# Splitting two row tiles of x first, residual copies on ScalarE, ten convolution taps moved

## The chip, the core and the metric

The kernel runs on one core of one Trainium2 chip. The metric is the device time of one execution in microseconds, median of the runs shown. TensorE, VectorE, ScalarE, GpSimd and SyncE run their own instruction streams and meet at semaphores; a transfer is issued on the queue of SyncE (SP) or ScalarE.

## What is computed

Two blocks follow each other on x of 256 tokens by 2048 channels, all in float32. The first block has two layers, and only it is touched by the change:

```python
hn = _rmsnorm(h, norm_g[i])
u = hn @ w_in[i]
a_val, a_glu, a_z, q, k, v, b_z = jnp.split(u, offs, axis=-1)
ya = _conformer_conv(a_val, a_glu, conv_w[i], ...)   # GLU, depthwise conv of width 31, LayerNorm, swish
ya = ya * silu(a_z)
yb = _window_attention(q, k, v, bias_band, sink[i]) * silu(b_z)
h = h + concatenate([ya, yb]) @ w_out[i]
e = _rmsnorm(p[i] @ w_pe[i], pe_g[i])
h = h + e * sigmoid(h @ w_pg[i])
```

The second block is one layer of forgetting attention and one of windowed attention, each with an input and an output projection.

## The kernel before

The activations lie channel-major: 16 row tiles of 128 channels by 256 tokens. Every product of float32 matrices is made of three reduced ones: x is split into a high and a low half (`a_hi`, `a_lo`; the next operand is `b_hi`, `b_lo`), and so is every weight (`w_hi`, `w_lo`). A weight is streamed in pieces of 256 rows by 512 columns through a ring of four slots (`RING`). For each piece, in this order: SP loads it into `stage` once the split of four pieces earlier is done (`load`, L286); ScalarE rounds it to `w_hi` (`rounded`, L1522); VectorE subtracts to get `w_lo` (`split`, L893); TensorE runs 24 matmuls over it (`gemm_piece`, L495, or L506 for the transposed kind). Eight pieces make a chunk of 512 output columns. The first block takes 156 pieces a layer: 11 input chunks (four of value and GLU columns, keys and values, two of q, two of gates, two of `z`), 4 pieces for `w_pe`, 8 x 4 for `w_out`, 4 x 8 for `w_pg`. All products take 577 pieces.

Each engine's program is a list written by hand: `chunk(hooks)` runs eight pieces and puts other work ("hooks") after piece i. VectorE's and ScalarE's chunk calls run three pieces behind the start of TensorE's chunks, since three splits come before the first call: VectorE's first call covers pieces 3 to 10, the next 11 to 18, and so on.

Start: ScalarE fetches `ident` and the norm gains, SP fetches x in four parts (`x_part`, L303) between the first weight loads, then 14 small constant arrays (`consts`, L308), then goes on loading weights. TensorE transposes x, four tiles to a part (`turn_x`, L665), parts 0 and 1 ahead of the first matmul, parts 2 and 3 inside the first chunk. ScalarE scales and rounds a tile from PSUM (`x_high`, L1531), VectorE makes the low half (`x_low`, L1073) and copies the part to the residual `h` (`x_new`, L1041 and L1045). TensorE waits for `operand_ready` ahead of every second piece. The sums of squares of h go ScalarE, VectorE (L948 to L955), TensorE (`stats`, L560), VectorE (`var`, L933), GpSimd (`inverse_root`, L1855 and L1857: a power, then a diagonal), TensorE (`spread_rs`, L572), VectorE (`take_rs`).

The depthwise convolution is VectorE's: 31 taps for 8 channel tiles are 248 steps of 128 x 256 (`taps`, L1139; the first tap of a tile is L1135), strewn between the splits. `conv_chunk(hooks, counts)` puts `counts[i]` taps after the split of its i-th piece and never more than are left (`spent`); after each pair of tiles `ln_add` (L1123) adds them to the mean. The last one releases TensorE's `ln_sum` (L719) in the second quarter of the attention half of `w_out`. The calls' counts stand in the diff. `evac` is the hook that takes a finished chunk out of PSUM, `gated` and `low_att` finish one half of the attention.

## Time and profile before

| | |
|---|---|
| median of 3 runs | 1775.8 us (1775.53 to 1776.24) |
| profiled execution, its own time | 1774.86 us |
| its span | 1773.1 us |
| TensorE busy | 1753.8 us (99%), 14349 matmuls |
| VectorE busy | 1309.7 us (74%) |
| ScalarE busy | 900.5 us (51%) |
| GpSimd busy | 38.1 us (2%) |
| from HBM | 320.4 MB, 182 GB/s over the span |

All times are from one profiled execution. A line of the timeline says when the first instruction of a group began, how long the group took, engine, line, operation, output and inputs, how many, and in brackets the idle time of the engine before it with what ended that. "L893" is line 893 of the kernel. Matmuls overlap, and their ends are modelled, so TensorE's busy share is high even where it runs below its peak; the starts of matmuls are the safer measure.

### The profile page before, as it was taken

The numbers are of one execution on the slowest core, as the hardware profiler recorded it, in microseconds if no ns is written. First come the engines' busy times: TensorE is split into PE (matmuls) and PEld (weight loads), VectorE is DVE, ScalarE is ACT, GpSimd is POOL, SyncE is SP. The second block draws the span as 40 slices with busy tenths as digits, with TensorE's granted clock in tenths as the row PEclk, the third lists the DMA queues.
The fourth block names the chain that finished last, engine by engine and source line by source line (L and its number), as shares of the span: only waits on it lengthen the run. The fifth ranks groups of instructions, "written<-read, shape, count | busy, mean of one in ns | idle before, by whom it ended". The sixth has DMA issues, their size and how long they took to land.

```text
span 1773.1 us, 35684 instructions
## 1 busy us (share of the span) xinstructions
PE 1753.8 (99%) x14349; PEld 1685.0 (95%) x14349; DVE 1309.7 (74%) x2087; ACT 900.5 (51%) x1326; POOL 38.1 (2%) x48
## 2 busy tenths in 40 slices
PE   8999999999999999999999999999999999999997
PEld 7999999999999999999999899999989999999886
DVE  7899899977679987998777765556565556666754
ACT  5433665545533465456565463545455443665553
POOL 0000000000000000000000110100100000000000
PEclk9999999999999999999999999999999999999999
DMA  7666655555666664556566666665655556555553
GB/s 233 188 206 195 191 145 177 195 186 194 196 188 204 195 201 145 157 194 197 180 200 184 206 200 181 192 187 181 193 159 167 191 179 192 156 158 172 168 193 131
DMA packets 200082, 326.07 MB, mean 184 GB/s; under 512 B 14911, under 2 KB 66319, under 8 KB 199821
## 3 DMA queue, kind: packets, MB, share of 16 engines
q1 hardware_dynamic: 197085, 320.85, 58.2%
q10 hardware_dynamic: 2864, 3.36, 0.6%
q8 instruction: 94, 1.54, 0.4%
q14 instruction: 39, 0.32, 0.1%
HBM read 320.42 MB, written 2.69 MB: 182 GB/s over the span
## 4 chain that ended last, share of the span: by engine, by line
PE 94%; DVE 4%; SPq 1%; ACT 0%; DMA 0%; issue 0%; DVEq 0%; ACTq 0%
PE g L495 75%; PE g L506 11%; PE att L596 2%; PE att L640 2%; PE att L620 2%; DVE w_lo L893 1%; DVE cacc L1139 1%; SPq L308 0%; PE att L495 0%; DMA stage<-in_w_in_dram 0%; PE att L784 0%; SPq L286 0%; ACT w_hi L1522 0%; PE att L572 0%; PE att L853 0%
## 5 line engine op out<-in xcount | busy, mean ns | idle before, releaser
L893 DVE TENSOR_TENSOR w_lo<-stage,w_hi 128x1024 fp32r<-128x1024 f32 x577 | 704.5, 1229 | 380.0 <-ACT w_hi L1522 379.1
L1522 ACT CAST w_hi<-stage 128x1024 fp32r<-128x1024 f32 x577 | 599.5, 1050 | 618.1 <-PE g L495 410.1
L495 PE MATMUL g<-a_hi,w_hi 128*128 128x256 f32 x2496 | 705.2, 283 | 3.0 <-DVE w_lo L893 2.0
L495 PE MATMUL g<-a_lo,w_hi 128*128 128x256 f32 x2496 | 695.9, 279 | 0.0
L495 PE MATMUL g<-a_hi,w_lo 128*128 128x256 f32 x2496 | 695.8, 279 | 0.0
L495 PEld LDWEIGHTS g<-a_hi,w_hi 128*128 128x128 f32 x2496 | 469.5, 188 | 13.0 <-issue 8.6
L495 PEld LDWEIGHTS g<-a_lo,w_hi 128*128 128x128 f32 x2496 | 472.7, 189 | 0.0
L495 PEld LDWEIGHTS g<-a_hi,w_lo 128*128 128x128 f32 x2496 | 469.2, 188 | 0.5 <-issue 0.2
L495 PE MATMUL g<-b_hi,w_hi 128*128 128x256 f32 x1440 | 404.4, 281 | 0.1
L495 PE MATMUL g<-b_lo,w_hi 128*128 128x256 f32 x1440 | 401.2, 279 | 0.0
L495 PE MATMUL g<-b_hi,w_lo 128*128 128x256 f32 x1440 | 401.2, 279 | 0.0
L495 PEld LDWEIGHTS g<-b_hi,w_hi 128*128 128x128 f32 x1440 | 270.6, 188 | 3.9 <-issue 2.9
L495 PEld LDWEIGHTS g<-b_lo,w_hi 128*128 128x128 f32 x1440 | 271.9, 189 | 0.0
L495 PEld LDWEIGHTS g<-b_hi,w_lo 128*128 128x128 f32 x1440 | 271.5, 189 | 0.1
L1139 DVE SCALAR_TENSOR_TENSOR cacc<-glu,cw,cacc 128x256 f32<-128x256 f32 x480 | 201.8, 478 | 0.2
L1531 ACT ACTIVATE u<-u,nbias 128x128 f32<-128x128 f32 (+1 forms) x192 | 88.1, 460 | 5.8 <-DVE nbias L1372 5.8
L1587 ACT COPY u<-att 128x384 f32<-128x384 f32 (+1 forms) x96 | 44.6, 516 | 53.4 <-PE att L620 53.4
L506 PE MATMUL g<-w_hi,a_hi 128*128 128x512 f32 (+1 forms) x192 | 68.9, 359 | 0.0
L506 PE MATMUL g<-w_lo,a_hi 128*128 128x512 f32 (+1 forms) x192 | 68.1, 355 | 0.0
L506 PE MATMUL g<-w_hi,a_lo 128*128 128x512 f32 (+1 forms) x192 | 67.8, 353 | 0.0
L506 PE MATMUL g<-w_hi,b_hi 128*128 128x512 f32 (+1 forms) x156 | 58.2, 373 | 0.0
L506 PE MATMUL g<-w_hi,b_lo 128*128 128x512 f32 (+1 forms) x156 | 57.5, 368 | 0.0
(230 smaller groups left out, 1359.9 us busy)
## 6 DMA issues: line engine op xcount, KB each, us to landing
stage<-in_fox_w_in_dram SPq DMA_DIRECT2D x128, 512.0 KB, 3.7
stage<-in_w_in_dram SPq DMA_DIRECT2D x112, 512.0 KB, 3.8
stage<-in_swa_w_in_dram SPq DMA_DIRECT2D x72, 512.0 KB, 3.8
stage<-in_w_in_dram SPq DMA_DIRECT2D x128, 256.0 KB, 3.1
stage<-in_w_out_dram SPq DMA_DIRECT2D x64, 512.0 KB, 4.3
stage<-in_w_pg_dram SPq DMA_DIRECT2D x64, 512.0 KB, 4.0
stage<-in_fox_w_out_dram SPq DMA_DIRECT2D x32, 512.0 KB, 4.3
stage<-in_swa_w_out_dram SPq DMA_DIRECT2D x32, 512.0 KB, 4.7
```

Of the source, the lines that this page charges most:

```text
L495: mm = pe.matmul(acc[:, j * S:(j + 1) * S], w[:, slot, c0 + j * P:c0 + (j + 1) * P], xx[:, k, :], start=st and m == 0 and j % 2 == 0, stop ...
L506: mm = pe.matmul(acc[:, at:at + width], xx[:, k, b * P:(b + 1) * P], w[:, slot, col:col + width], start=st and m == 0 and (kind == "N" or ...
L596: mm = pe.matmul(score_bank(j, len(pairs))[:, c:c + n], q_of(j, b), keys(j)[:, 0:n], start=b == 0, stop=True, skip_group_check=True)
L620: mm = pe.transpose((TB, SB)[j % 2][:, n * P:(n + 1) * P], uw[:, j, c + kb * P:c + (kb + 1) * P], ident[:, :])
L640: mm = pe.matmul(dst[half(j):half(j) + HD, at + first * P:at + S], values(j, kb), uw[:, j, n * P:(n + NB - first) * P], start=i % 2 == 0 a ...
L893: dve.tensor_tensor(w_lo[:, slot, :], stage[:, slot, :], w_hi[:, slot, :].bitcast(F32), ALU.subtract).then_inc(*t.inc("w_split"))
L1139: dve.scalar_tensor_tensor(out=cacc[:, c, :], in0=src, scalar=cw[:, c, l, k:k + 1], in1=cacc[:, c, :], op0=ALU.mult, op1=ALU.add).then_inc ...
L1522: act.copy(w_hi[:, slot, :], stage[:, slot, :]).then_inc(*t.inc("w_rounded"))
L1531: return act.activation(out, in_, func, **kw).then_inc(*t.inc(name))
L1587: act.copy(uw[:, j, 0:n], (TB, SB)[j % 2][:, 0:n]).then_inc(*t.inc("t_free"))
```

## The change

It has five parts.

1. x. Part 0 is fetched in two halves of two row tiles (`x_in0`, `x_in0b`). They are transposed, rounded and split separately, VectorE signals `operand_ready` after every two tiles, and TensorE waits for it ahead of every piece of the first chunk ("each"). TensorE runs nine matmuls on `ones` while nothing has arrived yet. The gains are fetched ahead of the identity.
2. The order on VectorE and ScalarE. The second weight piece is rounded and split between parts 0 and 1 of x.
3. Residual. Parts 0 and 1 of x, eight tiles, are copied to `h` by ScalarE, four copies of 128 x 512 (`x_keep`), behind the third rounded piece and ahead of the fetch of `p_in`. TensorE's `turn_x(2)` and `turn_x(3)` wait for them.
4. Taps, early. The third, fourth and fifth calls of `conv_chunk` lose 3, 5 and 3 taps.
5. Taps, late. The two calls with `normed_heads`, the second attention's and the last one gain 3, 2, 3 and 2; the last one had one more than was left, so it makes 18 where it made 15.

```diff
@@ SP
-            def x_part(g):
+            def x_part(event, at, n):
...
                     if l == 0 and n == 0:
-                        before = {g: x_part(g) for g in range(4)} | {4: consts}
+                        x_part("x_in0", 0, S)()
+                        before = {g: x_part(f"x_in{g}", g * CH, CH) for g in range(1, 4)} | {4: consts}
+                        before[1] = lambda: (x_part("x_in0b", S, S)(), x_part("x_in1", CH, CH)())
@@ TensorE
                 for n, i in enumerate(order[:pieces]):
-                    if ready and n % 2 == 0:
+                    if ready == "each" or ready and n % 2 == 0:
                         pe.wait_ge(*t.see("operand_ready"))
...
-            def turn_x(g):
+            def turn_x(g, tiles_=range(4), event=None):
                 def go():
-                    pe.wait_ge(*t.see(f"x_in{g}", 16))
+                    pe.wait_ge(*t.see(event or f"x_in{g}", 16))
                     if g >= 2:
-                        pe.wait_ge(*t.again("h_new", 1))
-                    for n in range(4):
+                        pe.wait_ge(*t.again("x_kept", 3 - g))
+                        t.skip("h_new")
+                    for n in tiles_:
...
+            def warm_up():
+
+                pe.wait_ge(*t.again("ones_set"))
+                for _ in range(WARM):
+                    pe.matmul(OB[:, 0:P], ones[:, :], ones[:, :], start=True, stop=True)
...
+            warm_up()
             pe.wait_ge(*t.see("ident_in", 16))
             turn_gains()
-            turn_x(0)()
+            turn_x(0, (0, 1))()
+            turn_x(0, (2, 3), "x_in0b")()
             turn_x(1)()
@@ VectorE
             split()
-            x_low(0)()
+            x_low(0, (0, 1))()
+            x_low(0, (2, 3))()
+            split()
             x_low(1)()
-            split()
-            x_new(0)()
-            x_new(1)()
             split()
...
                 STEADY = (2, 4, 3, 4, 4, 4, 4, 3)
                 conv_chunk({0: [evac(p1, val_glu(1))], 2: [glu_mul(1)]}, STEADY)
-                conv_chunk({0: [evac(p0, val_glu(2))], 2: [glu_mul(2)], 4: [p_low]}, STEADY)
-                conv_chunk({0: [evac(p1, val_glu(3))], 2: [glu_mul(3)]}, STEADY)
+                conv_chunk({0: [evac(p0, val_glu(2))], 2: [glu_mul(2)], 4: [p_low]}, (2, 3, 3, 3, 3, 4, 4, 3))
+                conv_chunk({0: [evac(p1, val_glu(3))], 2: [glu_mul(3)]}, (2, 3, 3, 3, 3, 3, 3, 3))
...
-                conv_chunk({0: [evac(p0, keys_values())]}, (2, 3, 3, 4, 4, 3, 3, 3), ahead={7: [q_in(p1)]})
+                conv_chunk({0: [evac(p0, keys_values())]}, (2, 2, 3, 3, 3, 3, 3, 3), ahead={7: [q_in(p1)]})
                 conv_chunk(attention(0), (2, 0, 0, 3, 0, 0, 3, 3), ahead={7: [q_in(p0)]})
-                conv_chunk(normed_heads(), (0, 0, 4, 4, 4, 4, 4, 2))
-                conv_chunk({0: [evac(p1, scaled(gate[:, :, :]))]} | attention(1), (0, 0, 0, 4, 0, 0, 3, 4),
+                conv_chunk(normed_heads(), (0, 0, 4, 4, 5, 5, 4, 3))
+                conv_chunk({0: [evac(p1, scaled(gate[:, :, :]))]} | attention(1), (0, 0, 0, 5, 0, 0, 4, 4),
                            after={1: [gated], 2: [low_att(0)]})
-                conv_chunk({0: [evac(p0, scaled(gate[:, :, :]))] + normed_heads()[0], 1: normed_heads()[1]}, (0, 0, 4, 4, 4, 4, 4, 2))
+                conv_chunk({0: [evac(p0, scaled(gate[:, :, :]))] + normed_heads()[0], 1: normed_heads()[1]}, (0, 0, 4, 4, 5, 5, 4, 3))
...
-                conv_chunk({}, (4, 4, 4, 4), HP)
+                conv_chunk({}, (5, 5, 4, 4), HP)
@@ ScalarE
+            fetch(vec_rows[0:depth * KT, :], norm_g.rearrange("l (k p) -> (l k) p", p=P), "gains_in")
             fetch(ident[:, :], ident_c, "ident_in")
-            fetch(vec_rows[0:depth * KT, :], norm_g.rearrange("l (k p) -> (l k) p", p=P), "gains_in")
...
+            def x_keep(g):
+
+                for n in (0, 2):
+                    act.wait_ge(*t.see("operand_ready"))
+                    dst = h[:, 4 * g + n:4 * g + n + 2, :].rearrange("p k s -> p (k s)")
+                    src = (G[1][:, n // 2 * CH:(n // 2 + 1) * CH], (SB, TB)[n // 2][:, :])[g]
+                    act.copy(dst, src).then_inc(*t.inc("x_kept" if n else "act_step"))
+
             rounded()
             act.wait_ge(*t.see("gains_done"))
-            x_high(0)()
+            x_high(0, (0, 1))()
+            x_high(0, (2, 3))()
+            rounded()
             x_high(1)()
             rounded()
-            rounded()
+            x_keep(0)
+            x_keep(1)
```

## Rows read from the trace of the kernel before

**Rows 1.** The page: the chain that ended last, by engine.
```profile
PE 94%; DVE 4%; SPq 1%; ACT 0%; DMA 0%; issue 0%; DVEq 0%; ACTq 0%
```

**Rows 2.** TensorE's waits, whole span: total us, times, longest.
```profile
PE g L495 <- DVE w_lo L893: 2.4, 5, 0.8
```

**Rows 3.** The timeline at the start, TensorE: start, us, engine, line, operation, count.
```profile
6.14 1.97 PE L665 MATMUL g<-ident,u 128*128 128x128 f32 x8
...
11.12 0.36 PE L495 MATMUL g<-a_hi,w_hi 128*128 128x256 f32 x1 [0.54 <-DVE a_lo L1073]
...
17.29 1.04 PE L665 MATMUL g<-ident,u 128*128 128x128 f32 x8
```

**Rows 4.** Transfers from 0 to 30 us: rate in 40 equal slices, one issue.
```profile
GB/s 0 0 49 201 287 270 322 363 380 363 361 392 404 367 363 366 374 370 344 319 185 163 150 236 249 310 344 348 365 344 359 344 195 223 373 96 7 23 190 369
...
p_in<-in_p_dram ACTq DMA_DIRECT2D x1, 256.0 KB, 6.4
```

**Rows 5.** The timeline from 15 to 49 us, of all engines.
```profile
15.12 0.38 SPq L286 DMA_DIRECT2D stage<-in_w_in_dram  x1
...
21.10 1.05 ACT L1522 CAST w_hi<-stage 128x1024 fp32r<-128x1024 f32 x1 [3.04 <-DMA stage<-in_w_in_dram]
22.18 1.23 DVE L893 TENSOR_TENSOR w_lo<-stage,w_hi 128x1024 fp32r<-128x1024 f32 x1 [2.86 <-ACT w_hi L1522]
...
42.66 0.61 PE L560 MATMUL att<-ones,q 128*128 128x1 f32 x4
...
48.05 0.61 POOL L1857 TENSOR_TENSOR diag<-ident,rs 128x256 f32<-128x256 f32 x1
48.72 0.70 PE L572 MATMUL att<-diag,ones 128*128 128x256 f32 x2
```

**Rows 6.** Windows: us, busy (x instructions) of PE, PEld, DVE, ACT, POOL; clock, DMA.
```profile
22.18:46.30 24.12, 23.87 (x199) 22.54 (x198) 23.32 (x38) 15.61 (x21) 0.00 (x0) 1.00 0.59 180
276.18:316.60 40.42, 40.42 (x349) 40.42 (x349) 40.19 (x71) 20.87 (x21) 0.00 (x0) 1.00 0.57 187
400.00:440.00 40.00, 40.00 (x355) 40.00 (x354) 27.38 (x32) 21.48 (x23) 0.00 (x0) 1.00 0.60 198
508.00:548.00 40.00, 40.00 (x342) 40.00 (x341) 36.05 (x63) 15.66 (x17) 0.00 (x0) 1.00 0.57 172
```

**Rows 7.** The timeline in the chunks with early taps, both layers.
```profile
107.90 0.36 PE L495 MATMUL g<-a_hi,w_hi 128*128 128x256 f32 x1 [0.84 <-DVE w_lo L893]
110.39 1.67 DVE L1139 SCALAR_TENSOR_TENSOR cacc<-glu,cw,cacc 128x256 f32<-128x256 f32 x4
111.98 1.22 DVE L893 TENSOR_TENSOR w_lo<-stage,w_hi 128x1024 fp32r<-128x1024 f32 x1
...
119.87 0.39 PE L495 MATMUL g<-a_hi,w_hi 128*128 128x256 f32 x1 [0.54 <-DVE w_lo L893]
...
587.10 0.38 PE L495 MATMUL g<-b_hi,w_hi 128*128 128x256 f32 x1
```

**Rows 8.** The timeline around the late chunks, up to the piece after them.
```profile
210.65 1.23 DVE L893 TENSOR_TENSOR w_lo<-stage,w_hi 128x1024 fp32r<-128x1024 f32 x1 [1.15 <-ACT w_hi L1522]
...
266.79 0.88 DVE L1139 SCALAR_TENSOR_TENSOR cacc<-glu,cw,cacc 128x256 f32<-128x256 f32 x2
267.80 1.23 DVE L893 TENSOR_TENSOR w_lo<-stage,w_hi 128x1024 fp32r<-128x1024 f32 x1
...
276.18 1.23 DVE L893 TENSOR_TENSOR w_lo<-stage,w_hi 128x1024 fp32r<-128x1024 f32 x1 [1.68 <-ACT w_hi L1522]
277.77 0.28 PE L495 MATMUL g<-a_hi,w_hi 128*128 128x256 f32 x1
...
738.75 0.38 PE L495 MATMUL g<-b_hi,w_hi 128*128 128x256 f32 x1
```

**Rows 9.** The timeline at the sum of the layer norm.
```profile
315.70 0.88 DVE L1123 TENSOR_TENSOR mean<-mean,cacc 128x256 f32<-128x256 f32 x2
316.93 0.59 PE L719 MATMUL att<-mean,ones 128*128 128x256 f32 x2
```

More of the change, by code:

```diff
@@ L46 @@
 APART = 240
+WARM = 9
 REL0 = S - 1
@@ L231, in two_blocks @@
         names = """w_rounded w_split w_used gemm_free operand_ready
-            dve_step act_step pool_step x_in0 x_in1 x_in2 x_in3 gains_in gains_turned gains_done x_turned consts_in consts2_in tables_in rel_ready rel_out rel_bias_done
+            dve_step act_step pool_step x_in0 x_in0b x_in1 x_in2 x_in3 x_kept gains_in gains_turned gains_done x_turned consts_in consts2_in tables_in rel_ready rel_out rel_bias_done
             bias_in scored s_free maxed weights_ready pt_done t_free att_done normed ob_free mb_free
@@ L298, in _ @@
             t.skip("att_done", (depth * 2 + 4) * GH)
-            def x_part(g):
+            def x_part(event, at, n):
                 def go():
-                    cols = slice(g * CH, (g + 1) * CH)
+                    cols = slice(at, at + n)
                     sp.dma_start(u[:, :].rearrange("p (b d) -> p b d", b=NB)[:, :, cols],
-                                 x[0].rearrange("(b p) d -> p b d", p=P)[:, :, cols]).then_inc(*t.dma(f"x_in{g}"))
+                                 x[0].rearrange("(b p) d -> p b d", p=P)[:, :, cols]).then_inc(*t.dma(event))
                 return go
@@ L666, in go @@
                     mm.then_inc(*t.inc("x_turned"))
-                    t.skip("h_new")
                 return go
+            def warm_up():
+                pe.wait_ge(*t.again("ones_set"))
+                for _ in range(WARM):
+                    pe.matmul(OB[:, 0:P], ones[:, :], ones[:, :], start=True, stop=True)
             def turn_gains():
@@ L689, in turn_consts @@
                 t.skip("rel_bias_done")
+            warm_up()
             pe.wait_ge(*t.see("ident_in", 16))
             turn_gains()
-            turn_x(0)()
+            turn_x(0, (0, 1))()
+            turn_x(0, (2, 3), "x_in0b")()
             turn_x(1)()
-            pe.wait_ge(*t.again("ones_set"))
+            t.skip("x_kept", 2)
             for l in range(depth):
@@ L748, in _ @@
                 p0, p1 = flip, 1 - flip
-                chunk("T", A, p0, ready=True, work={15: [stats()]} if l else {3: [turn_x(2)], 5: [turn_x(3)], 11: [turn_consts]})
+                chunk("T", A, p0, ready=True if l else "each", work={15: [stats()]} if l else {3: [turn_x(2)], 5: [turn_x(3)], 11: [turn_consts]})
                 chunk("T", A, p1, work={3: [spread_rs()]} if l else {2: [stats()], 6: [spread_rs()]})
@@ L1065, in _, with x_low @@
             XY = ((a_hi, a_lo), (b_hi, b_lo))
-            def x_low(g):
+            def x_low(g, tiles_=range(4)):
                 def go():
                     dve.wait_ge(*t.see("x_turned"))
-                    for n in range(4):
+                    for n in tiles_:
                         k = 4 * g + n
@@ L1074, in go @@
                                                  in1=XY[0][0][:, k, :].bitcast(F32), op0=ALU.mult,
-                                                 op1=ALU.subtract).then_inc(*t.inc("operand_ready" if n == 3 else "dve_step"))
+                                                 op1=ALU.subtract).then_inc(*t.inc("operand_ready" if n % 2 else "dve_step"))
                 return go
@@ L1610, in _, with x_high @@
             f_(es[:, 0, 0:1], ones[:, 0:1], ACT.Copy)
-            def x_high(g):
+            def x_high(g, tiles_=range(4)):
                 def go():
                     act.wait_ge(*t.see("x_turned"))
-                    for n in range(4):
+                    for n in tiles_:
                         k = 4 * g + n
@@ L1617, in x_high, with x_there @@
                 return go
+            def x_keep(g):
[4 more added lines that the diff above has]
+                    act.copy(dst, src).then_inc(*t.inc("x_kept" if n else "act_step"))
             rounded()
             act.wait_ge(*t.see("gains_done"))
-            x_high(0)()
+            x_high(0, (0, 1))()
+            x_high(0, (2, 3))()
+            rounded()
             x_high(1)()
             rounded()
-            rounded()
+            x_keep(0)
+            x_keep(1)
+            def x_there():
+                act.wait_ge(*t.again("x_kept"))
             def rel_table():
@@ L1628, in rel_table @@
                 fetch(rel_d, relt, "rel_out")
-            tail = {1: [x_high(2)], 2: [x_high(3)], 3: [h_wait, square(0, h)],
-                    4: [h_wait, square(1, h)], 5: [h_wait, square(2, h)], 6: [h_wait, square(3, h)], 7: [rel_table]}
+            tail = {1: [x_high(2)], 2: [x_high(3)], 3: [x_there, square(0, h)],
+                    4: [square(1, h)], 5: [h_wait, square(2, h)], 6: [h_wait, square(3, h)], 7: [rel_table]}
             for l in range(depth):
```

## Prediction

> **What bounds the kernel now.** I read the chain that ended last first: TensorE holds nearly all of it [rows 1]. The second view was TensorE's waits over the whole span: the largest is 2.4 us for `w_lo`, VectorE's half of the weight split [rows 2]. So TensorE is the bound, there is little idle time to win, and a shift can pay only where TensorE waits for VectorE or for the start. Third, the timeline of these places, engine by engine, asking of every wait what VectorE did before it. A weight piece is 24 matmuls; VectorE splits it about four pieces before TensorE takes it, and its taps lie between the splits. Pieces are counted from 0.
>
> **The start.** The first matmul is at 11.12; the eight transposes of tiles 0 to 3 begin at 6.14 and take 0.25 us each, where eight later ones take 0.13 each [rows 3]. The change feeds TensorE sooner. `gains_in` and `ident_in` only swap places on ScalarE's queue, so transposing still begins near 6.1, but after nine warm-up matmuls at the full rate, four transposes instead of eight: 1.97 - 4 x 0.13 = 1.4 us less ahead of `a_hi`. (0.25 and 0.13 us are the engine's two clock levels, 1.2 and 2.4 GHz; it had idled until 5.9.) VectorE then does two `a_lo` steps (0.40 apart) before the first signal instead of four: the first matmul comes 0.8 to 1.5 us earlier, near 9.9.
>
> I give this no credit, since it is taken back twice. TensorE sums the squares at 42.66 and spreads the root at 48.72; the root's diagonal, on GpSimd, begins at 48.05 and takes 0.61, so it is there at 48.66 and the spread follows at once [rows 5]. VectorE leads up to this: from its split of piece 4 at 22.18 to `var` at 46.3 it is busy 23.32 of 24.12 us [rows 5, 6]. All of it hangs on piece 4's weights, for which ScalarE waits until 21.10 [rows 5]. A TensorE that is ahead only waits longer at 42.7. The two `x_new` that go to ScalarE lie ahead of 22.18, where VectorE idles 2.86 us anyway [rows 5], and save nothing.
>
> So the start gains what piece 4's weights gain. The rate of all transfers falls from some 360 GB/s to 185, 163, 150 and 236 in the four slices of 0.75 us from 15.0 [rows 4]: small constants and `p_in` are on then. `p_in` is 256 KB and takes 6.4 us to land [rows 4]; its issue sits behind ScalarE's whole prologue, which now holds four copies waiting for `operand_ready`. I put these at 14 to 16.5 (third weight piece rounded at 14.1, four steps near 0.6), so `p_in` leaves near 16 instead of 13 and its packets arrive when piece 4's are nearly through. Bounds: nothing if it still competes; the whole dip, 4 x 360 - 734 = 706, over 360, times 0.75 = 1.5 us, at most. By bytes `p_in` is 0.26 MB / 360 GB/s = 0.7. SP's one more issue (0.4 to 0.5 us, as the one at 15.12) is covered by a backlog: piece 4 is issued at 15.12 and used at 21.10 [rows 5]; without that cover it costs its 0.5. I take **-0.8** (0.5 to -1.5), nearest to the bytes.
>
> The Trainium skill, "DMA: Bandwidth & Descriptors", section "Queues, rings and completion order", says that each DMA engine serves the queues with work in turn, packet by packet. By it a later `p_in` would take half of each engine while piece 4 lands, and this term would be near -0.3; no row here shows the two together.
>
> Covered edits: ScalarE's four residual copies (2.4 us) lie before it waits for pieces 3 and 4 (3.04 us idle before 21.10, rows 5); if that cover went, they would delay rounding by as much. `turn_x(2)` and `(3)` now wait for `x_kept` on ScalarE; behind that wait is the GEMM itself. By the estimate above the first comes near 15.2, when TensorE arrives at 15.5. "each" adds waits for tiles long done.
>
> **The early chunks.** Four taps and a split take 111.98 - 110.39 + 1.14 = 2.73 us; a tap is 0.40 [rows 7]. A piece takes TensorE 2.72 at its quick pace, so there VectorE is the slower one once it adds evacuations. TensorE waits 0.84 before 107.90 and 0.54 before 119.87, and shorter before three or four others [rows 7]. The cuts: the first call with `STEADY` keeps its 28 taps, the next loses 3, the third 5, and the one with `keys_values` 3. Following each piece in the first layer (VectorE's split end minus the taps cut so far; TensorE's start the later of the split and of its last piece's end):
> - piece 30: split 0.40 earlier, wait 0.53 to 0.13.
> - piece 32: 1.20 earlier, and the mean's add (0.46) moves one piece later, wait 1.17 to 0; piece 33 gets that add, wait 0 to 0.16.
> - piece 36: VectorE is 1.2 us earlier, TensorE 1.17 - 0.16 + 0.40 = 1.4 earlier, so it waits 0.97 where it waited 0.81.
> - pieces 38 and 44: 0.35 and 0.26 go.
>
> Sum 0.40 + 1.17 - 0.16 - 0.16 + 0.35 + 0.26 = **-1.9**. Here a wait is what its piece takes beyond the usual 2.72 or 2.79; that is 0.3 more than the view prints, which counts from the modelled end of the last matmul. Its mark is a long first matmul (0.36 to 0.39 against 0.28, rows 7, 8). In the second layer TensorE is 1 to 4 us behind the splits until piece 192 of all, and short waits follow: one is before the matmul of 587.10 [rows 7], 0.38; two more like it are 0.26 each: **-0.9**, all gone since 1.2 us of cut lies ahead of them.
>
> **The late chunks.** Three taps enter the call with the first `normed_heads`. VectorE is idle 1.15 us before 210.65, waiting for ScalarE [rows 8], and 3 x 0.40 = 1.19 fits. Two enter `attention(1)`, also before waits. The three in the second `normed_heads` call have no such cover. VectorE's last two taps start at 266.79, 0.88 us, and the split of piece 83 starts at 267.80: 0.2 us free [rows 8]. The remaining 1.0 goes through a chain without slack: split, `gated`, ScalarE's rounding, `low_att`, the evacuation of `z`, its Silu, ScalarE's rounding of piece 84, VectorE's split at 276.18 [rows 8]. That ends at 277.42 and TensorE starts the piece at 277.77; 0.3 us of slack, 1.0 later: it waits 0.8. From there VectorE is busy 40.19 of 40.42 us up to `ln_sum` [rows 6], and the last call (`(5, 5, 4, 4)`, 18 taps where 15 were left) adds 1.2 more. The mean is ready at 316.58 and TensorE uses it at 316.93 [rows 9]: slack 0.2. VectorE comes 1.0 + 1.2 = 2.2 later, TensorE by itself 0.8, so the rest is waited out there and at the next sum (`ln_bc`, which TensorE already waits for). **+2.2** for this layer. In the second, the matmul at 738.75 is of the long kind (0.38), so TensorE already waits at this piece [rows 8]; nothing is left to absorb: **+2.2** again. If the tail of the chain were late by the taps alone, it would be 1.0 each.
>
> **Sum.** -0.8 - 1.9 - 0.9 + 4.4 = +0.8; unrounded late terms (2.16) make it +0.7. The profiled execution took 1774.9 us, of which its span is 1773.1; the median of the runs shown is 0.9 above it, 1775.8. I add the difference to the median: **1776.5**. With the terms' bounds (0.5 to -1.5; early -2.0 to -3.2; late 2.0 to 4.6) it goes from -2.7 to +3.1.
>
> **The rivals.**
> - *The late taps are hidden* because VectorE's chain to piece 84 gives way somewhere (it has 1.68 us idle before 276.18, though behind ScalarE). Against: each link starts when the one before it ends. Then -0.8 - 1.9 - 0.9 = -3.6: 1772.2. Chance 0.12.
> - *The pace tips the wrong way: slower.* Equal matmuls run at two paces: 355 in 40 us from 400, 342 in 40 us from 508, at one granted clock [rows 6]. The pace changes only at waits and inserted work. New waits at pieces 84 and at `ln_sum` could put the long quick stretch from 380 to 502 on the slow one: 1067 matmuls x 4.5 ns = 4.8 us, 1781.3. It decides from about 600 matmuls that change over. For it: two new waits. Against: the stretch begins with its own wait, for the spread root, which stays. Chance 0.10. The same in the other direction (265 to 317 and 328 to 370, some 700 matmuls, -3.2 with the rest +0.7: 1773.3 or, in both layers, 1770): 0.06.
> - *The clock falls back after the warm-up.* TensorE idles near 5.3 to 6.1, 6.6 to 6.9 and 7.4 to 8.7, and with the first two pieces at 1.2 GHz (2.7 us more each) the 0.8 us of the start and the 0.7 us of waiting at 42.7 don't cover it: about +5, 1780.7. Against: in the kernel before, transposes alone lead from the slow rate at 6.14 to a first piece at the full one [rows 3]. Chance 0.04.
> - The Trainium skill, "TensorE: Matmul & The Clock Gate", Part 4, says that transposes don't count as work for the clock. By that rule this rival would be likely; the trace disagrees.
> - The forecast: 0.68.
>
> **How the numbers follow.** About 0.2% (3.55 us) is what a measurement of this kernel can tell from no change: 1772.25 to 1779.35. Faster: the hidden taps at the edge (0.10 of 0.12) and the kind pace (0.05): 0.15. Slower: bad pace 0.10 and clock 0.04, and 0.01 of the forecast: 0.15. Same: 0.70. The range takes in the forecast's bounds and the near part of both rivals: 1772.0 to 1780.0.
>
> **What would show it.** First matmul near 9.9, but the sum of squares only 0.8 us earlier, with a wait of TensorE before it. Waits for `w_lo` gone at pieces 32, 38 and 44, still there at 36 (0.97). `p_in` issued near 16. A wait near 0.8 at piece 84, then one on VectorE's mean at `ln_sum`, twice. It would be wrong if VectorE's split of piece 84 were not later against TensorE, if piece 4 landed at 21.1 as before, or if the counts in 40 us of the long stretches changed.

## The result, and the profile after

The changed kernel takes 1778.5 us, the kernel before, beside it on the same chip, 1776.3 us (medians of 22 runs each); ratio 1.0015, 95% interval 1.0009 to 1.0021. So by the ratio it is slower by 2.7 us (1.6 to 3.7; the two medians lie 2.2 apart), within the 0.2% that the forecast called the same. The profiled execution took 1777.69 us, its span is 1775.9.

The changed kernel's lines are numbered otherwise: `split` is L904, `rounded` L1532, `gemm_piece` L498, the root's diagonal L1881. First its chain and TensorE's waits (for what, total us, times, longest), then the start, which answers [rows 3]:

```profile
PE 53%; DVE 4%; issue 0%; ACT 0%; DMA 0%; ACTq 0%; DVEq 0%
PE att L730 <- DVE mean L1133: 1.7, 2, 0.8
PE g L498 <- DVE w_lo L904: 1.6, 4, 0.5
PE att L735 <- DVE mean L1228: 0.5, 1, 0.5
PE att L563 <- DVE q L966: 0.4, 1, 0.4
PE att L575 <- POOL diag L1881: 0.3, 1, 0.3
...
1.34 4.21 PE L677 MATMUL att<-ones 128*128 128x128 f32 x18 [1.34 <-POOL ones L1872]
5.72 0.79 PE L669 MATMUL g<-ident,u 128*128 128x128 f32 x4
7.77 0.66 PE L669 MATMUL g<-ident,u 128*128 128x128 f32 x4 [1.26 <-DMA u<-in_x_dram]
9.64 1.97 PE L669 MATMUL att<-ident,u 128*128 128x128 f32 x8 [1.22 <-DMA u<-in_x_dram]
11.26 0.56 PE L498 MATMUL g<-a_hi,w_hi 128*128 128x256 f32 x1
```

The chain is followed through little more than half the span, so it says only that TensorE leads. The waits say more: the 2.4 us for `w_lo` [rows 2] are down to 1.6, and four new rows are there: the mean of the layer norm (twice 0.8), its second sum, the sum of squares and the root. The warm-up ran, the first two lots of four transposes took 0.20 and 0.17 us each, and then, after two waits for x, the eight at 9.64 took 0.25 each: the 1.2 GHz level again, and the granted clock is 0.61 from 9 to 11 us and 0.77 from 11 to 15. The first matmul comes at 11.26, where it came at 11.12 [rows 3].

The rates and `p_in` (answering [rows 4]), and the way to the first root ([rows 5]), from issue to spread:

```profile
GB/s 0 0 96 249 276 318 298 255 320 322 330 385 365 350 381 389 391 369 358 355 215 171 207 159 183 319 378 352 369 356 340 354 198 49 134 307 281 8 0 81
p_in<-in_p_dram ACTq DMA_DIRECT2D x1, 256.0 KB, 5.8
...
16.02 13.41 SPq L287 DMA_DIRECT2D stage<-in_w_in_dram  x12
22.32 1.05 ACT L1532 CAST w_hi<-stage 128x1024 fp32r<-128x1024 f32 x1 [3.33 <-DMA stage<-in_w_in_dram]
43.88 0.61 PE L563 MATMUL att<-ones,q 128*128 128x1 f32 x4 [0.35 <-DVE q L966]
49.70 0.61 POOL L1881 TENSOR_TENSOR diag<-ident,rs 128x256 f32<-128x256 f32 x1
50.37 0.70 PE L575 MATMUL att<-diag,ones 128*128 128x256 f32 x2 [0.33 <-POOL diag L1881]
```

Piece 4's load is issued 0.9 us later (16.02 for 15.12) and rounded 1.2 later (22.32 for 21.10); the sum of squares follows 1.2 later, the root's diagonal and the spread 1.65. `p_in`, whose issue was put near 16, leaves at 14.86. The chain from piece 4 to the root is the one that the forecast named; only it moved the wrong way. The dip of the rate has not gone: 215, 171, 207, 159, 183.

The taps (answering [rows 6 to 9]): what is left of the early waits, piece 84, the layer norm's sum, and piece 240, its counterpart in the second layer; then the windows of the two long stretches.

```profile
120.20 0.39 PE L498 MATMUL g<-a_hi,w_hi 128*128 128x256 f32 x1 [0.27 <-DVE w_lo L904]
...
276.84 1.23 DVE L904 TENSOR_TENSOR w_lo<-stage,w_hi 128x1024 fp32r<-128x1024 f32 x1 [1.68 <-ACT w_hi L1532]
278.12 0.39 PE L498 MATMUL g<-a_hi,w_hi 128*128 128x256 f32 x1 [0.49 <-DVE w_lo L904]
318.48 0.70 PE L730 MATMUL att<-mean,ones 128*128 128x256 f32 x2 [0.84 <-DVE mean L1133]
740.43 0.39 PE L498 MATMUL g<-b_hi,w_hi 128*128 128x256 f32 x1 [0.48 <-DVE w_lo L904]
...
400.00:440.00 40.00, 40.00 (x356) 40.00 (x355) 28.33 (x33) 21.70 (x24) 0.00 (x0) 1.00 0.58 192
508.00:548.00 40.00, 40.00 (x340) 39.95 (x339) 35.22 (x61) 15.65 (x16) 0.00 (x0) 1.00 0.54 166
```

The waits near 107.9 and in the second layer near 587 are gone, the one of piece 36 is left, and piece 84 and `ln_sum` wait as foretold. The windows of the long stretches are the same within two matmuls (356 and 340, for 355 and 342): the pace did not tip in this execution.

To see where time goes I take from a trace when each piece's last matmul has been counted, and subtract what the kernel before has there. "Piece 12, +1.80" means that TensorE is 1.80 us later at the end of piece 12. The kernels of the middle columns come below.

| piece | changed | changed, again | taps alone | start alone | taps in gaps | constants later |
|---|---|---|---|---|---|---|
| 12 | +1.80 | +2.23 | +0.77 | +2.51 | +0.95 | -0.12 |
| 20 | +2.65 | +3.08 | +1.63 | +2.52 | +1.81 | +0.73 |
| 44 | -0.28 | +0.14 | -1.06 | +2.39 | -0.85 | -2.00 |
| 80 | -0.30 | +0.14 | -1.06 | +2.38 | -0.76 | -1.99 |
| 104 | +1.65 | +2.31 | +1.09 | +2.19 | -0.76 | +0.18 |
| 168 | +1.66 | +7.04 | +5.83 | +6.93 | -0.75 | +4.91 |
| 204 | +0.75 | +6.12 | +4.91 | +6.94 | -1.66 | +4.00 |
| 264 | +3.07 | +8.49 | +7.26 | +6.96 | -1.55 | +6.36 |
| 324 | +3.06 | +13.06 | +7.59 | +6.96 | -1.56 | +10.93 |
| 576 | +2.82 | +12.84 | +7.60 | +6.97 | -2.11 | +10.71 |

The first column is the whole result: +2.65 up to piece 20 (0.85 of it between 12 and 20, where the kernel before ran at the quick pace and this one at the slow), early taps back to -0.28, late taps of the first layer to +1.65, the second layer -0.9 and +2.3. That execution matches the ratio's 2.7.

### The profile page after: what moved, and what is told of

It is laid out like the page before. It is cut to its first block, busy times and chain, and to the rows that moved or that the text cites. A ratio compares the mean times of both kernels' runs of the same rounds, so it can differ in the third digit from the quotient of the medians.

```text
span 1775.9 us, 35725 instructions
## 1 busy us (share of the span) xinstructions
PE 1757.5 (99%) x14367; PEld 1688.7 (95%) x14367; DVE 1306.4 (74%) x2084; ACT 902.8 (51%) x1330; POOL 38.1 (2%) x48
## 4 chain that ended last, share of the span: by engine, by line
PE 53%; DVE 4%; issue 0%; ACT 0%; DMA 0%; ACTq 0%; DVEq 0%
PE g L498 38%; PE g L509 10%; DVE w_lo L904 2%; PE att L599 1%; DVE cacc L1149 1%; PE att L643 1%; PE att L623 1%; PE att L795 0%; DMA turned<-q 0%; PE att L864 0%; ACT w_hi L1532 0%; ACTq L1520 0%; PE att L575 0%; DVE glu L1226 0%; PE att L563 0%
## 5 line engine op out<-in xcount | busy, mean ns | idle before, releaser
L904 DVE TENSOR_TENSOR w_lo<-stage,w_hi 128x1024 fp32r<-128x1024 f32 x577 | 703.7, 1227 | 378.3 <-ACT w_hi L1532 377.2
L1532 ACT CAST w_hi<-stage 128x1024 fp32r<-128x1024 f32 x577 | 599.7, 1050 | 618.8 <-PE g L498 435.2
L498 PE MATMUL g<-a_hi,w_hi 128*128 128x256 f32 x2496 | 705.1, 283 | 1.3 <-DVE w_lo L904 0.8
L498 PE MATMUL g<-a_lo,w_hi 128*128 128x256 f32 x2496 | 696.2, 279 | 0.0
L498 PE MATMUL g<-a_hi,w_lo 128*128 128x256 f32 x2496 | 696.1, 279 | 0.0
L498 PEld LDWEIGHTS g<-a_hi,w_hi 128*128 128x128 f32 x2496 | 469.5, 188 | 10.4 <-issue 7.0
L498 PEld LDWEIGHTS g<-a_lo,w_hi 128*128 128x128 f32 x2496 | 472.4, 189 | 0.0
L498 PEld LDWEIGHTS g<-a_hi,w_lo 128*128 128x128 f32 x2496 | 470.7, 189 | 0.5 <-issue 0.2
L498 PE MATMUL g<-b_hi,w_hi 128*128 128x256 f32 x1440 | 404.0, 281 | 0.5 <-DVE w_lo L904 0.5
L498 PE MATMUL g<-b_lo,w_hi 128*128 128x256 f32 x1440 | 401.1, 279 | 0.0
L498 PE MATMUL g<-b_hi,w_lo 128*128 128x256 f32 x1440 | 401.1, 279 | 0.0
L498 PEld LDWEIGHTS g<-b_hi,w_hi 128*128 128x128 f32 x1440 | 270.9, 188 | 3.7 <-issue 2.9
L498 PEld LDWEIGHTS g<-b_lo,w_hi 128*128 128x128 f32 x1440 | 272.1, 189 | 0.0
L498 PEld LDWEIGHTS g<-b_hi,w_lo 128*128 128x128 f32 x1440 | 271.0, 188 | 0.1
```

The costliest lines, as they stand in the source:

```text
L498: mm = pe.matmul(acc[:, j * S:(j + 1) * S], w[:, slot, c0 + j * P:c0 + (j + 1) * P], xx[:, k, :], start=st and m == 0 and j % 2 == 0, stop ...
L904: dve.tensor_tensor(w_lo[:, slot, :], stage[:, slot, :], w_hi[:, slot, :].bitcast(F32), ALU.subtract).then_inc(*t.inc("w_split"))
L1532: act.copy(w_hi[:, slot, :], stage[:, slot, :]).then_inc(*t.inc("w_rounded"))
```

## The experiments

On the chips of these runs the spread was wider (the kernel before took 1773.4 to 1786.4 us), and on one of them the times fall into groups some 4.7 us apart: 15 of 30 runs of before lie from 1773.4 to 1776.3, 12 from 1778.5 to 1781.3, 3 from 1785.2 to 1786.4. (The 35 of another chip spread as far, with less clear gaps.) The table shows what that is: between pieces 104 and 168, and again from 264 to 324, some executions lose 4 to 5 us and others nothing. So I read terms of a microsecond from the piece ends, outside these stretches, and the ratios only for the sum.

**The taps alone.** Kernel before, with all tap counts of the changed one.

> The kernel before with the tap counts of the changed kernel, its start left as it was. Theory A (the splits of the first layer's pieces 30 to 44 set the time, as forecast): early cuts -1.9 and -0.9, late taps +2.2 twice, +1.6 us against the kernel before; TensorE arrives at piece 44 1.9 us earlier than before. Theory B (the early cuts are worth in themselves what the changed kernel shows between pieces 20 and 44, from +2.65 to -0.28): -2.9 -0.9 +2.2 +2.3 = +0.7 us, and TensorE 2.9 us earlier at piece 44.

Ratio 1.0005 (0.9992 to 1.0018), +1.5 us by the medians. The late terms are +2.15 (piece 80 to 104) and +2.35 (204 to 264), the second layer's early term -0.92. The first layer's can't be read from this trace alone: it also came to piece 20 1.63 us late, and a kernel with the old taps that was nearly as late there (+1.17, the pace run below) had worked off 0.9 us of that by piece 44, in the same waits. Against it the cuts are worth 1.3 to 1.8 us. That is nearer to theory A (1.9) than to B (2.9), by one trace against one.

**The start alone.** Changed kernel, with the old tap counts.

> The changed kernel with the tap counts of the kernel before: the new start alone. Theory A (the later start is hidden, because without the cuts VectorE's splits of pieces 30 to 36 set TensorE's time and VectorE has caught up by then): piece 4 lands 1.2 us later than before and TensorE is some 2.6 us late at piece 20, but only 0 to 0.4 us at piece 44; total 0 to +0.4 us against the kernel before. Theory B (start and taps add): the changed kernel's +2.7 less the taps' +1.6, so +1.1 us. Theory C (it was all the start): +2.7 us.

Ratio 1.0011 (0.9995 to 1.0028). Theory A fell: of 2.52 us at piece 20, 2.39 are left at piece 44, because here VectorE is late too and its waits move along. The part that costs is thus the new start, about 2.2 us up to piece 104; the rest up to 6.97 is one long stretch at the other pace. That is near the 2.7 of theory C, yet the late taps have their price too (above): start and taps don't simply add, since the early cuts take back a good part of the start's lateness. Its start rows show the half clock level once more (transposes 0.25 us), and piece 4:

```profile
15.84 2.94 SPq L287 DMA_DIRECT2D stage<-in_w_in_dram  x6
23.18 1.05 ACT L1532 CAST w_hi<-stage 128x1024 fp32r<-128x1024 f32 x1 [3.31 <-DMA stage<-in_w_in_dram]
```

**The constants later.** Changed kernel; the 14 small fetches go behind piece 4's load.

```diff
-before = {g: x_part(f"x_in{g}", g * CH, CH) for g in range(1, 4)} | {4: consts}
+before = {g: x_part(f"x_in{g}", g * CH, CH) for g in range(1, 4)} | {5: consts}
```

> The changed kernel with SyncE's fourteen small constant fetches issued behind the load of weight piece 4 instead of ahead of it. Theory A (piece 4's landing, set by when its load is issued, leads to the sum of squares): the load is issued near 9.3 us instead of 16.0, piece 4 lands near 15, the first sum of squares and the spread root come 2 to 2.8 us earlier (TensorE's waits in pieces 4 to 11 of the changed kernel sum to 2.8), and 1.5 to 2.5 us of it are left at the end: about -2 us against the changed kernel, +0.7 against the kernel before. Theory B (the transfers' rate sets it, not the order of issue): the small fetches and p_in then delay piece 5 to about 23.8, the chain leads from there, and the gain is 0 to -0.5 us.

```profile
10.47 1.01 SPq L309 DMA_DIRECT2D cacc<-in_pe_g_dram  x1
16.68 1.06 ACT L1532 CAST w_hi<-stage 128x1024 fp32r<-128x1024 f32 x1
19.02 1.05 ACT L1532 CAST w_hi<-stage 128x1024 fp32r<-128x1024 f32 x1 [1.29 <-DMA stage<-in_w_in_dram]
23.16 1.05 ACT L1532 CAST w_hi<-stage 128x1024 fp32r<-128x1024 f32 x1 [1.62 <-DMA stage<-in_w_in_dram]
45.80 0.61 POOL L1881 TENSOR_TENSOR diag<-ident,rs 128x256 f32<-128x256 f32 x1
```

The rows are SyncE's first constant, ScalarE's rounding of pieces 3, 4 and 5, and the root's diagonal. Piece 4 is issued 6.8 us earlier, at 9.19, and rounded 3.3 earlier, at 19.02 (22.32 in the changed kernel); piece 5 is rounded at 23.16 (24.71). The diagonal begins at 45.80 (49.70), and TensorE neither waits at the sum of squares nor at the root. At piece 12 it is 1.9 to 2.6 us ahead of the three traces with the changed start, at piece 104 1.5 to 2.1. Piece 4 did not land near 15, as theory A had it, and piece 5 came nearly as late as theory B said, but the gain is theory A's: piece 4's landing is the path, and it hangs on SyncE's order. The ratio, 1.0008 (0.9994 to 1.0022), hides it: this trace had both long stretches at the slow pace.

**One fetch fewer.** Changed kernel with part 0 of x in one transfer (`x_in0b` gone), steps in halves kept.

> The changed kernel with part 0 of x fetched in one piece again; its transposes, rounding and low halves stay in two steps. Theory A (SyncE's issues in a row set when piece 4's load is issued, and one more costs its own time): the load of piece 4 is issued at 15.1 to 15.3 us instead of 16.0, and ScalarE rounds it 0.7 to 1.2 us earlier than in the changed kernel (22.3 to 23.2 there). Theory B (the transfers set it, the residual order or p_in): issue at 15.1 but landing as late as before, 22.3 to 23.2.

```profile
14.94 4.60 SPq L287 DMA_DIRECT2D stage<-in_w_in_dram  x8
22.06 1.05 ACT L1531 CAST w_hi<-stage 128x1024 fp32r<-128x1024 f32 x1 [4.76 <-DMA stage<-in_w_in_dram]
```

**`p_in` later.** Changed kernel with the fetch of `p_in` behind the rounding of piece 4 (it leaves at 23.41, ahead of piece 5's rounding, not near 26).

> The changed kernel with ScalarE's fetch of p_in behind its rounding of piece 5, near 26 us, instead of at 14.9. Theory A (p_in takes its share of the DMA engines while piece 4 lands, packet by packet): piece 4 is issued at 16.0 as in the changed kernel and rounded 0.3 to 0.7 us earlier, 21.8 to 22.5 where it was 22.3 to 23.2. Theory B (p_in is through before piece 4's packets matter): no difference, 22.3 to 23.2.

```profile
15.57 4.54 SPq L287 DMA_DIRECT2D stage<-in_w_in_dram  x7
21.89 1.05 ACT L1532 CAST w_hi<-stage 128x1024 fp32r<-128x1024 f32 x1 [3.48 <-DMA stage<-in_w_in_dram]
```

Neither takes the delay away. Each kernel ran once (1777.48 and 1777.50 us); in the traces they are 1.53 and 1.36 us behind before at piece 12, and 2.60 and 2.63 at the end. Rounding of piece 4 begins at 20.19 to 21.31 in the four traces that have the start of before, at 22.32, 22.75 and 23.18 in three with the changed start, at 22.06 and 21.89 here. On the mean the changed start issues the load 0.9 us later and rounds the piece 2.0 later. Without the extra fetch the load goes at 14.94, as early as before, yet the rounding is only 0.7 us earlier, between the two theories; with `p_in` out of the way it is 0.9 earlier, as theory A had it. Executions of one start differ by about as much, so the shares of the two are open, and so is whether both together would make up the 2.0. With the constants behind piece 4 it is rounded at 19.02, earlier than with either start: that shows how much the landing hangs on what is issued ahead of it, not which edit made it late.

In both traces TensorE's first piece ended earlier than in the kernel before (by 0.60 and 1.10 us), since its matmuls came 0.11 us apart from 10.9 and 10.2 us on, and then it waited 1.6 us for the `a_lo` that VectorE makes behind piece 4.

**The taps in the gaps.** Kernel before, with the eleven early taps cut as in the changed kernel, and put where VectorE waits for ScalarE (the changed calls):

```diff
-conv_chunk(attention(0), (2, 0, 0, 3, 0, 0, 3, 3), ...)
-conv_chunk(normed_heads(), (0, 0, 4, 4, 4, 4, 4, 2))
-conv_chunk(... | attention(1), (0, 0, 0, 4, 0, 0, 3, 4), ...)
+conv_chunk(attention(0), (2, 0, 0, 3, 0, 0, 7, 3), ...)
+conv_chunk(normed_heads(), (0, 0, 4, 4, 4, 4, 4, 4))
+conv_chunk(... | attention(1), (1, 0, 0, 4, 0, 0, 7, 4), ...)
```

> The kernel before with the eleven early taps cut as in the changed kernel (3, 5 and 3 in the third, fourth and fifth calls), but put where VectorE waits for ScalarE: four more after the split of the seventh piece of the first attention call, two more at the end of the first call with normed heads, one at the start and four at the seventh piece of the second attention call; the later calls are left alone. Theory A (a tap costs nothing where VectorE idles 1.2 to 2.0 us for ScalarE's rounding): -1.9 -0.9 = -2.8 us against the kernel before. Theory B (taps ahead of a rounding delay the chain from attention to piece 84 as late taps do): the late terms come back, up to +4.4, so +1.6 us.

Ratio 0.9983 (0.9968 to 0.9998), -2.6 us by the medians: theory A. Against the taps alone, which start alike, it saves 2.15 us in the first layer and 2.24 in the second, and nothing else but for the pace. VectorE at such a spot, and all of TensorE's waits behind the start:

```profile
234.82 2.85 DVE L1139 SCALAR_TENSOR_TENSOR cacc<-glu,cw,cacc 128x256 f32<-128x256 f32 x7
238.10 1.22 DVE L893 TENSOR_TENSOR w_lo<-stage,w_hi 128x1024 fp32r<-128x1024 f32 x1 [0.43 <-ACT w_hi L1522]
...
PE g L495 <- DVE w_lo L893: 0.5, 1, 0.5
```

Seven taps are followed by 0.43 us of waiting for ScalarE, where the kernel before waits 2.00 after three: the four more cost nothing. The price of the late taps was their place, not their number.

**Both.** The same with the constants behind piece 4.

> The kernel before with two edits: SyncE's fourteen constant fetches behind the load of weight piece 4, and the eleven taps moved into VectorE's idle spots as in the run with taps in the gaps. Theory A (both terms are terms of TensorE's waits and add): taps -2.3 to -2.8 us; the start of the kernel before shows waits of 0.5 us at the sum of squares and the root where weights are late, and up to 1.5 us less at the first chunk, so -1 more: -3.5 us, 0 to -1 if TensorE's slow clock at the start is what holds it. Theory B (the constants behind piece 4 delay pieces 5 and 6 as much): -2.5 us, as with the taps alone.

Ratio 0.9997 (0.9980 to 1.0013), not told from before, with the groups of 4.7 us in it. By the trace: at piece 12 it is 0.24 us behind before (+0.95 with the taps in the gaps alone), from piece 44 to 168 -1.6, at the end -2.41. The old start gains less from the constants (0.7 us) than the changed one (2), since TensorE is at the 1.2 GHz level for its first piece and is itself the bound there. The run with other numbers (below) bears this out: same start, first piece at the full rate, and it is 0.85 us ahead of before at piece 12.

**The warm-up without gaps.** Changed kernel, with five more warm-up matmuls ahead of each of the second and third lots of transposes.

> The changed kernel with five more warm-up matmuls in each of TensorE's two waits for the quarters of x, so that it has no idle time of a microsecond ahead of the eight transposes. Theory A (the late weights of piece 4, through VectorE, set the sum of squares and the root, so that TensorE's speed before that doesn't count): transposes at 0.13 instead of 0.25 us and the first matmuls at 0.11 instead of 0.21, TensorE's first piece ends 1.5 to 2.5 us earlier, its waits at the squares and the root grow by as much, and the time is that of the changed kernel within 0.4 us. Theory B (the fall of the clock costs its own time): -1.5 to -2.5 us against the changed kernel.

```profile
9.50 1.07 PE L669 MATMUL att<-ident,u 128*128 128x128 f32 x8
10.32 0.36 PE L498 MATMUL g<-a_hi,w_hi 128*128 128x256 f32 x1
10.53 0.28 PE L498 MATMUL g<-a_hi,w_lo 128*128 128x256 f32 x1
...
23.91 1.04 ACT L1534 CAST w_hi<-stage 128x1024 fp32r<-128x1024 f32 x1 [4.88 <-DMA stage<-in_w_in_dram]
27.05 0.39 PE L498 MATMUL g<-a_hi,w_hi 128*128 128x256 f32 x1 [3.41 <-DVE a_lo L1086]
1109.54 0.50 PE L509 MATMUL g<-w_hi,a_hi 128*128 128x512 f32 x1 [2.64 <-DVE w_lo L906]
1100.00:1120.00 20.00, 17.36 (x101) 14.87 (x100) 8.12 (x7) 6.76 (x7) 0.00 (x0) 0.91 0.53 157
q8 instruction: 112, 1.84, 0.4%
```

The transposes took 0.13 us each and the first matmuls 0.11, and piece 0 ended 1.7 us earlier than in the changed kernel. Yet at piece 12 TensorE was 3.5 us behind before: piece 4 landed later still (23.91) and TensorE waited for what VectorE makes behind it. So its speed ahead of piece 4 buys nothing (theory A), but the time was not the changed kernel's: 1791 us, ratio 1.0064 (1.0041 to 1.0086). At piece 12 it was 1.0 to 1.7 us behind the three traces with the changed start: TensorE waited 3.41 us for `a_lo`, and behind that wait the granted clock is 0.50 from 28.2 to 31.5, its matmuls 0.21 apart. Two further jumps of 4.2 and 4.5 us stand in the trace near 1109 and 1212, at the end of two rounds of the forgetting attention's loop. TensorE halts there for 2.7 us each, and behind it the granted clock dips (0.91 in the window), which is the rest. The row names `w_lo` as the releaser, but that piece's split was ready 6.1 us before the halt, so it was something else; and 112 packets of instructions are on record where every other kernel here has 94. That longer code ahead of the loop makes the loop fetch its code again is a guess, not tried by itself: this kernel has 38 more matmuls there than the kernel before, while the changed kernel with 18 more and the pace run with 20 more transposes show neither the packets nor the halts. The long stretches at the slow pace account for the rest.

**The changed kernel again.**

> The changed kernel once more, unaltered, beside the others on their chip. Theory A (its +2.7 us come from its own waits): the piece ends match those of its first trace within 1 us up to piece 104, apart from the pace of whole stretches: piece 4 rounded near 22.5, TensorE waiting near 0.5 us at the squares and at the root, waits of 0.8 at piece 84 and 1.1 at the layer norm's sum. Theory B (the start is chance): piece 4 rounded near 21.2 and no waits at the squares and the root.

Theory A for the start and the taps: the table's second column keeps within 0.66 us of the first up to piece 104, with waits of 0.7 us at the sum of squares and 0.3 at the root. Then it loses 4.7 us up to piece 168 and 4.6 from 264 to 324: both long stretches at the slow pace. Ratio 1.0012 (0.9994 to 1.0030), which on this chip alone would not be told from no change.

```profile
400.00:440.00 40.00, 40.00 (x342) 40.00 (x341) 27.30 (x32) 20.69 (x23) 0.00 (x0) 1.00 0.58 188
```

**The pace.** Kernel before, with a group of four transposes, `tune`, at six places, and the root of the convolution half a slot later.

```diff
+def tune():
+    for _ in range(4):
+        pe.transpose(TB[:, 0:P], ident[:, :], ident[:, :])
...
-                chunk("T", A, 0)
+                chunk("T", A, 0, work={0: [tune]})
```

> The kernel before with four needless transposes of the identity into a free PSUM bank at six places where TensorE's matmuls come every 0.118 us, and the spread root of the first block's convolution half one slot later, so that TensorE doesn't wait for it. In the traces so far the four transposes of p_in, met at the slow pace, were followed by the quick one (0.113 us) in 8 of 8 cases, and a spread root that TensorE didn't wait for by the slow one in 18 of 18. Theory A (the pace is a state of TensorE's queue that an interruption sets anew, whatever the work): the stretches behind the transposes go quick, 14, 41 and 16 pieces in the first block's layers and 16 pieces of each of three rounds and 32 behind the last in the forgetting attention; 0.11 us a piece less 0.5 us for each group of transposes: -7 us against a kernel before whose long stretch was quick, -11 against one whose long stretches were slow. Theory B (the pace depends on what the stretch reads, a contention of SBUF or of weights' arrival): the pace stays and the transposes cost 0.5 us each, ten of them, +5 us.

Ratio 0.9974 (0.9958 to 0.9989), 4.6 us faster. Half of each theory. Behind the forgetting attention all four stretches went quick, where all eleven traces without transposes there have them slow: from piece 348 to 480 this kernel gains 7.8 us. In the first block all five groups left the pace slow, so both long stretches were slow, and the groups cost 0.45 us each.

**The pace, kept to where it worked.** Both edits of before, and `tune` in the forgetting block alone.

> The kernel before with the constants behind weight piece 4, the eleven taps in VectorE's idle spots, and four needless transposes of the identity behind the first half piece of the chunk that follows the attention in the forgetting block, in its three rounds and after the last. Theory A (the transposes set the quick pace there, as they did with these same four places before, 7.8 us between pieces 348 and 480): about -2 for the first two edits and -7.8, so -10 us against the kernel before, whatever pace the first block's two long stretches take (each 4.6 to 4.8 us when slow, in either kernel by chance). Theory B (the pace there was chance too): -2.5 us, or -2.5 and part of the 7.8.

**Other numbers.** As that, with `tune(2 + l)`, `tune(5 + l)` and `tune(1)` in the first block's layers.

> As the one before, and in the first block's layers other numbers of needless transposes behind the places that four left slow: two and three behind the second sum of the layer norm, five and six behind the spread root of the convolution half (which comes a slot later, unwaited for), one behind the root of the second layer. Theory A (which pace follows hangs on how the number of transposes shifts TensorE's two instruction streams against each other): at least one of these numbers gives the quick pace, its stretch 0.11 us a piece shorter: 14 pieces, 41 pieces, 16 pieces. Theory B (behind an unwaited root the pace is slow in these chunks whatever comes between): all of them slow, the time that of a kernel whose two long stretches are slow, so about 9 us above the one with the transposes in the forgetting block alone at its best, and some 2 us for the extra transposes.

The two kernels take 1764.9 and 1765.0 us, ratios 0.9937 (0.9924 to 0.9951) and 0.9942 (0.9928 to 0.9955): 11.2 and 10.3 us faster than before by the ratios, 10.3 and 10.2 by the medians; the changed kernel was not run beside them. The first is what its theory A said. The other numbers gained nothing on top. One window, in the forgetting block's last chunks, of before and then of the first of them:

```profile
1350.00:1390.00 40.00, 40.00 (x342) 40.00 (x341) 23.07 (x23) 17.97 (x20) 0.00 (x0) 1.00 0.58 189
...
1350.00:1390.00 40.00, 40.00 (x355) 40.00 (x355) 22.65 (x23) 18.21 (x24) 0.00 (x0) 1.00 0.61 196
```

Same work, same granted clock, 355 matmuls for 342. In all three kernels with transposes there the block is 7.8 us shorter. In the layers two, five and six transposes were followed by the quick pace, one, three and four by the slow one. Theory A of the last run holds for at least one number of each long stretch: five and six gave 41 quick pieces each, behind a root that TensorE doesn't wait for. Each number was seen once (four: five times), so this is no rule yet; what the number shifts is not shown.

## Why the forecast was right, and where it was not

The time (1776.5 forecast, 1778.5 measured, 2.7 above before where 0.7 was said) fell in the range and in the likeliest class. By the steps:

- **Start, -0.8: wrong in sign.** It was +1.7 at piece 12 (three traces of the changed start 2.18 behind before on the mean, four traces of the old one 0.51). The step that failed is the term of piece 4's weights: a gain of 0.8 from `p_in`, and "SP's one more issue is covered by a backlog". They landed later, rounding at 22.75 for 20.77 on the mean. The issue at 15.12 was read with the use at 21.10 and taken for slack; but the row of 21.10 has ScalarE idle for 3.04 us waiting for this very transfer, so the use followed the landing. A queue that ran thin while the small constants were issued, at half the rate [rows 4], would explain why a later issue costs; that is argued, and without the extra issue most of the lateness stayed. The gain put on `p_in` was a guess from bytes and from an issue near 16 that came at 14.86; the fetch at 23.41 took 0.9 us of the 2.0 off, in one trace. The forecast's bound above, +0.5, missed too.
- **No credit for the earlier matmul: right.** The first matmul came at 11.26, not 9.9 (10.02 to 11.26 in the traces that have this start or a variant of it), as the clock fell back between the warm-up and the eight transposes. That rival (chance 0.04, +5 us) was right in its mechanism and wrong in its price: the slow clock hardly shows at the end, since the sum of squares waited for VectorE anyway; the three traces whose first piece ran early (one fetch fewer, `p_in` later, warm-up without gaps) were 1.4 to 3.5 us behind at piece 12 all the same. What spoke against it, "transposes alone lead to the full rate", rested on one trace: of seven traces with the transposes of before, two have the first piece at the full rate, and in five its matmuls come every 0.21 us up to about 15 us. The Trainium skill, "TensorE: Matmul & The Clock Gate", Part 4, has transposes not counting as work for the clock; the five agree, the two don't.
- **Early cuts, -1.9 and -0.9.** Second layer: -0.91, exact. First layer: between 1.3 and 1.8 against a kernel nearly as late, 2.3 to 2.7 between the start alone and the whole change. By pieces, in the changed kernel: 30 lost all 0.53 (0.40 was said), 32 lost 1.11 (1.17), 33 got no wait (0.16 was said), 36 kept 0.57 (0.97 was said), 38 and 44 lost 0.40 and 0.26. Piece 28 lost 0.35, which the sum had left out. A TensorE on the slow pace from piece 12 to 20 gave VectorE some of the slack that the steps for 33 and 36 denied it.
- **Late taps, +2.2 a layer.** +1.95 and +2.32 in the changed kernel, 2.15 and 2.35 with the taps alone. The route too: 0.76 at piece 84 (0.8), 1.03 at `ln_sum` beyond before's (1.2), the rest at the next sum. The rival in which they are hidden is refuted, and the run with taps in the gaps shows what hiding them takes.
- **The pace.** In the forecast a rival of 0.10 for the change. It is real and of the size given (4.6 to 4.8 us a stretch), but it belongs to the execution, not to the change: the kernel before has it in its own times. The two new waits did not decide it. The forecast's stretch starts with the wait for the root at 379.7; of 24 such waited roots in twelve traces 15 led to the quick pace and 9 to the slow one. The spread starts 0.216 to 0.227 us behind the matmul before it; at 0.226 or more all six led to the slow pace, below it 15 of 18 to the quick one. So a few nanoseconds may decide; nothing here sets them on purpose.

One reading was off without harm: 2.4 us for `w_lo` is TensorE's largest wait behind the start, not over the whole span, where 5.9 us for the gains come first.

So the sum's +0.7 became +2.7 in the start and the first layer's early cuts together: -2.7 was said for both, and at piece 44 the changed kernel stands at -0.28 and +0.14 in its two traces. The two can't be parted sharply, as they meet in the same waits. All other taps came to +3.4 where +3.5 was said. That the time still fell in the range is owed to the range's width: the miss of the start uses up most of what it had above the forecast.

## What to carry to other kernels

A transfer's slack is what lies between its landing and its use; where the engine that uses it idles for it, there is none, however early it was issued. Small fetches ahead of a large one hold up its issue, by about 0.46 us each here, even when the bytes are nothing; about half of that showed in the landing (3.3 of 6.8 us). Work moved off one tight place should go to where its engine visibly waits for another: the same eleven taps cost 4.4 us in one place and nothing in another. Where the times of a kernel fall into groups, compare the ends of the same work in several traces before giving a microsecond to a cause.

## What the runs showed of the hardware

Long runs of equal matmuls have two paces, 0.1133 and 0.1178 us, at one granted clock, and keep the one they start with until other work interrupts them. Behind the first block's roots that TensorE did not wait for the pace was slow in every trace (unless transposes followed); in the second block one such root was followed by the quick pace in all fourteen, so this is no rule. Behind one that it waited for some 0.1 us it was either, from run to run. That makes the groups of 4.7 us. Four needless transposes (0.45 us) behind the attention set the quick one 12 times in 12, against none of 44 without them, which is worth 0.11 us for each piece that follows there. The clock in the first 15 us also differed between executions: with the transposes of before, TensorE's first matmuls came 0.11 us apart in two traces and 0.21 us apart up to 14.6 to 15.5 us in five. The granted clock of a window reads 1.00 there in all seven, so early on the spacing of the matmuls is the safer measure. And in one kernel, 20 more matmuls ahead of a loop than in the changed kernel went with 18 more packets of instructions and halts of 2.7 us at two turns of the loop.
